# An eighteenth place for expert matrices, one place for overflow matrices, and a reordered expert round

## The reference, cut to what matters

```python
g_sel = jnp.argmax(g_logits, axis=-1)                 # one of 8 groups per token
top_v, top_i = lax.top_k(e_logits, MOE_TOP_K)         # 2 of its 8 experts
gate = p_group[:, None] * jax.nn.softmax(top_v, axis=-1)
...
hid = jax.nn.silu(xb @ w_gate_e[e]) * (xb @ w_up_e[e])   # 64 experts, 1024 -> 256
return hid @ w_down_e[e]                                 # 256 -> 1024
...
return jnp.zeros_like(h2).at[tok].add(ys * wt[:, None])
```

## Time and profile before

| | |
|---|---|
| median of 3 runs | 1522.63 us |
| the profiled execution | 1525.64 us |
| its span, first to last instruction | 1524.0 us |
| PE busy | 1452.7 us (95%) |
| VectorE, ScalarE, GpSimd busy | 526.9, 337.8, 6.7 us |
| DMA over the span | 347.40 MB, mean 228 GB/s |
| mean granted TensorE clock | 0.991 |

### The profile page before, as it was taken

The page is one execution under the profiler, slowest core; times in us unless marked ns, Lnnn a source line. Parts: engine busy times, 40 slices in busy tenths (PEclk is TensorE's granted clock), DMA queues, the critical chain, the costliest instruction groups (busy, mean ns, idle before and its releaser), DMA issues.

```text
span 1524.0 us, 29271 instructions
## 1 busy us (share of the span) xinstructions
PE 1452.7 (95%) x12680; PEld 1232.9 (81%) x12680; DVE 526.9 (35%) x1284; ACT 337.8 (22%) x749; POOL 6.7 (0%) x72
## 2 busy tenths in 40 slices
PE   8999999999999999999999999997999998998887
PEld 6868889978888888888888888886777777776765
DVE  0536164211344430228854541014222332232322
ACT  2153401241100000121555530102111111111111
POOL 0000000000000000000000000000000000000000
PEclk9999999999999999999999999998999999999999
DMA  8333334223444423544334443384999999999995
GB/s 329 132 139 114 135 112 157 70 98 138 138 165 139 149 76 152 231 145 160 115 135 137 141 139 138 138 358 157 420 423 424 423 424 424 424 423 423 424 424 224
DMA packets 58336, 347.40 MB, mean 228 GB/s; under 512 B 12416, under 2 KB 13536, under 8 KB 18656
## 3 DMA queue, kind: packets, MB, share of 16 engines
q1 hardware_dynamic: 55536, 339.20, 57.2%
q10 hardware_dynamic: 2672, 6.33, 1.3%
HBM read 413.21 MB, written 1.49 MB: 272 GB/s over the span
## 4 chain that ended last, share of the span: by engine, by line
PE 88%; DMA 6%; DVE 2%; issue 2%; ACT 1%; SPq 0%; DVEq 0%; ACTq 0%
PE bank L399 37%; PE bank L1049 9%; PE bank L450 9%; PE bank L413 6%; PE bank L1069 5%; PE bank L1080 4%; PE bank L1093 4%; DMA ring<-w_gate_e_dram 4%; PE bank L466 2%; DMA work<-w_gate_e_dram 2%; PE bank L555 1%; PE bank L511 1%; PE bank L927 1%; DVE work L1698 1%; PE bank L701 1%
## 5 line engine op out<-in xcount | busy, mean ns | idle before, releaser
L399 PE MATMUL bank<-hT,ring 128*128 128x256 f32 x2016 | 443.5, 381 | 1.9 <-DVE hT L1698 1.8
L399 PEld LDWEIGHTS bank<-hT,ring 128*128 128x128 f32 x2016 | 382.9, 191 | 56.8 <-issue 6.7
L1707 DVE TENSOR_TENSOR xT<-xT,bank 128x512 f32<-128x512 f32 x100 | 68.8, 688 | 320.7 <-PE bank L1069 210.8
L399 PE MATMUL bank<-work,ring 128*128 128x256 f32 x704 | 153.5, 380 | 0.0
L399 PEld LDWEIGHTS bank<-work,ring 128*128 128x128 f32 x704 | 133.8, 190 | 18.5 <-issue 1.0
L450 PE MATMUL bank<-work,ring 128*128 128x256 f32 x608 | 131.6, 379 | 0.0
L450 PEld LDWEIGHTS bank<-work,ring 128*128 128x128 f32 x608 | 115.8, 190 | 15.4
L1049 PE MATMUL bank<-work 128*32 128x128 f32 x2144 | 113.9, 273 | 11.7 <-issue 9.3
L1049 PEld LDWEIGHTS bank<-work 128*32 128x32 f32 x2144 | 104.3, 110 | 24.0 <-issue 23.6
L1049 PEld LDWEIGHTS bank<-ring,work 128*32 128x32 f32 x1568 | 74.5, 112 | 21.6 <-issue 21.6
L1049 PE MATMUL bank<-ring,work 128*32 128x128 f32 x1568 | 81.4, 278 | 10.5 <-issue 6.8
(11 more groups left out here) (357 smaller groups left out, 1718.7 us busy)
## 6 DMA issues: line engine op xcount, KB each, us to landing
work<-w_up_e_dram SPq DMA_DIRECT2D x33, 1024.0 KB, 23.6
work<-w_down_e_dram SPq DMA_DIRECT2D x33, 1024.0 KB, 26.0
work<-w_gate_e_dram SPq DMA_DIRECT2D x30, 1024.0 KB, 25.8
ring<-w_gate_e_dram SPq DMA_DIRECT2D x26, 1024.0 KB, 26.3
ring<-w_down_e_dram SPq DMA_DIRECT2D x23, 1024.0 KB, 25.1
ring<-w_up_e_dram SPq DMA_DIRECT2D x23, 1024.0 KB, 25.7
ring<-w_up_dram SPq DMA_DIRECT2D x22, 1024.0 KB, 4.9
ring<-w_gates_dram SPq DMA_DIRECT2D x20, 1024.0 KB, 4.9
```

Source lines behind the costliest of these rows:

```text
L399: m = mm(b[:, j * SEQ:(j + 1) * SEQ], w[:, k, j * P:(j + 1) * P], tile(k), start=(k == 0), stop=(k == kt - 1))
L1707: return v.tensor_tensor(dst, a, b, ALU.add)
```

## The change

- The work area is packed again: the routing scratch `rt` moves into `scratch`, `rtx` and `over_add` lie under the place of the expert outputs, `selw_t` under `sel_t`, and the area holds nine 2048-column places for matrices where it held eight. `sq` becomes an expert place as well: 18 places.
- The overflow matrices keep only `hT`. GpSimd's load of turn n now waits for the product of turn n - 1.
- In every round scatter 0 and 1 of the round before stand ahead of gate, and scatter 2 and 3 between gate and up. VectorE adds all four before `gated`.
- During the three waits of the routing TensorE runs 6, 11 and 10 spare products of 128 columns (`keep_running`) into the bank that is written next.
- The last round's down matrices are loaded in halves, first the first half of each, then the second, with a semaphore for each half; `out_of_hidden(r, 0)` waits for the first halves, `out_of_hidden(r, 1)` for the second.
- The output is stored in four parts, each when its additions are done.

```diff
-        wide = area(8704, 8, SLOT)
+        wide = area(6656, 9, SLOT)
...
-        expert_slots = ([wide[:, n, :] for n in range(2, 8)] + [con_sb[:, mask_at:mask_at + SLOT]]
-                        + [ring[(len(UNITS) + n) % RING][:, :] for n in range(RING)] + [wide[:, n, :] for n in range(2)]
-                        + [scratch[:, 0:SLOT]])
+        expert_slots = ([wide[:, n, :] for n in range(3, 9)] + [con_sb[:, mask_at:mask_at + SLOT]]
+                        + [ring[(len(UNITS) + n) % RING][:, :] for n in range(RING)] + [wide[:, n, :] for n in (1, 2)]
+                        + [scratch[:, 0:SLOT], wide[:, 0, :], sq[:, :]])
...
-        over_slots = [hT[:, :, :].rearrange("p k t -> p (k t)"), sq[:, :]]
+        over_slot = hT[:, :, :].rearrange("p k t -> p (k t)")
...
+            def keep_running(times):
+
+                n = len(product)
+                pe.wait_ge(free_sem[n % 8], n // 8)
+                for _ in range(times):
+                    mm(bank[n % 8][:, 0:P], ones, ident, start=True, stop=True)
+
+            keep_running(6)
             pe.wait_ge(S("chosen"), nth("chosen"))
...
+            keep_running(11)
             pe.wait_ge(S("places"), nth("places"))
...
+            keep_running(10)
             pe.wait_ge(S("sel_ready"), 1)
...
+                if r >= 1:
+                    scatter(r - 1, 0)
+                    scatter(r - 1, 1)
                 weights_here("w_gate_e", r)
                 into_hidden("w_gate_e", r, 0)
                 into_hidden("w_gate_e", r, 1)
                 if r == 0:
                     token_rows()
                 if r >= 1:
-                    scatter(r - 1, 0)
-                    scatter(r - 1, 1)
+                    scatter(r - 1, 2)
+                    scatter(r - 1, 3)
                 weights_here("w_up_e", r)
                 into_hidden("w_up_e", r, 0)
                 into_hidden("w_up_e", r, 1)
-                if r >= 1:
-                    scatter(r - 1, 2)
-                    scatter(r - 1, 3)
...
+            overflow_here("w_down_e", GROUPS - 1)
+            for n in range(2):
+                pe.wait_ge(S(f"last_down_landed{n}"), 16 * len(own_experts(GROUPS - 1)))
+                out_of_hidden(GROUPS - 1, n)
...
+                elif u == SLOTS - 3:
+                    sp.wait_ge(product_ready, made("ynt", 7))
                 elif u == SLOTS - 1:
-                    sp.wait_ge(product_ready, made("ynt", 7))
+                    sp.wait_ge(product_ready, made("ssq", 1))
+                elif u == SLOTS - 2:
+                    sp.wait_ge(product_ready, made("out2", 3))
...
+                if (name, r) == ("w_down_e", GROUPS - 1):
+                    sp.dma_start(half_down(expert_slots[u % SLOTS], 0), half_down(A[name][e], 0))\
+                        .then_inc(S("last_down_landed0"), 16)
...
+            for e in own_experts(GROUPS - 1):
+                sp.dma_start(half_down(expert_slots[UNIT_OF["w_down_e", e] % SLOTS], 1), half_down(A["w_down_e"][e], 1))\
+                    .then_inc(S("last_down_landed1"), 16)
             for n in range(4):
+                part = slice(2 * n, 2 * n + 2)
                 sp.wait_ge(bank_free("scatter", GROUPS - 1, n), used("scatter", GROUPS - 1, n))
-            sp.dma_start(out, xT[:, :, :]).then_inc(S("stored"), 16)
+                sp.dma_start(out[:, part, :], xT[:, part, :]).then_inc(S(f"stored{n}"), 16)
...
-                if turn_ >= 2:
-                    pool.wait_ge(product_ready, made(READER[KINDS[(turn_ - 2) % len(KINDS)]], (turn_ - 2) // len(KINDS), 1))
+                if turn_ >= 1:
+                    pool.wait_ge(product_ready, made(READER[KINDS[(turn_ - 1) % len(KINDS)]], (turn_ - 1) // len(KINDS), 1))
```

More of the change, by code:

```diff
@@ L223, in build @@
         selw = area(5376, SEQ)
[L224 to L229, removed]
-        wide = area(8704, 8, SLOT)
+        selw_t = area(5120, SEQ)
+        d_row = area(5632, 2, SEQ)
+        g_row = area(6144, 2, SEQ)
+        rtx = area(3840, 640)
+        over_add = area(4480, EXPERTS)
+        wide = area(6656, 9, SLOT)
         scratch = sb("scratch", [P, 3072])
@@ L234, in build @@
         root2 = scratch[:, 1024:3072]
+        rt = scratch[:, 2048:3072].rearrange("p (t n) -> p t n", t=TT)
         row_buf2 = tmp[0:TT * SSD_HEADS, 1, 0:P]
@@ L310, in expert_weights @@
             if j == OWN:
-                return over_slots[over_turn(name, r) % 2]
+                return over_slot
             return expert_slots[UNIT_OF[name, min(FIRST_OF[r] + j, FIRST_OF[r + 1] - 1)] % SLOTS]
         expert_landed = [S(f"expert_weights_landed{n}") for n in range(SLOTS)]
-        over_landed = [S(f"overflow_weights_landed{n}") for n in range(2)]
+        over_landed = S("overflow_weights_landed")
         def b3(ap, n, inner):
@@ L1038, in weights_here, with overflow_here @@
                     pe.wait_ge(expert_landed[u % SLOTS], 16 * (u // SLOTS + 1))
-                turn_ = over_turn(name, r)
-                pe.wait_ge(over_landed[turn_ % 2], 16 * (turn_ // 2 + 1))
+                overflow_here(name, r)
+            def overflow_here(name, r):
+                pe.wait_ge(over_landed, 16 * (over_turn(name, r) + 1))
             def into_hidden(name, r, n):
@@ L1120, in _ @@
                 turn(r, 1)
-                weights_here("w_down_e", r)
-                out_of_hidden(r, 0)
-                out_of_hidden(r, 1)
+                if r + 1 < GROUPS:
+                    weights_here("w_down_e", r)
+                    out_of_hidden(r, 0)
+                    out_of_hidden(r, 1)
+            overflow_here("w_down_e", GROUPS - 1)
+            for n in range(2):
+                pe.wait_ge(S(f"last_down_landed{n}"), 16 * len(own_experts(GROUPS - 1)))
+                out_of_hidden(GROUPS - 1, n)
             for n in range(4):
@@ L1172, in _, with half_down @@
                     sp.dma_start(pos_sb[:, :], A["pos"]).then_inc(S("late_loads"), 16)
+            def half_down(a, n):
+                return a.rearrange("p (f m) -> p f m", f=2)[:, :, n * 512:(n + 1) * 512]
             ring0 = 7
@@ L1186, in _ @@
                     sp.wait_ge(product_ready, made(READER[before_name], before_r, 1))
-                sp.dma_start(expert_slots[u % SLOTS], A[name][e]).then_inc(expert_landed[u % SLOTS], 16)
+                if (name, r) == ("w_down_e", GROUPS - 1):
+                    sp.dma_start(half_down(expert_slots[u % SLOTS], 0), half_down(A[name][e], 0))\
+                        .then_inc(S("last_down_landed0"), 16)
+                else:
+                    sp.dma_start(expert_slots[u % SLOTS], A[name][e]).then_inc(expert_landed[u % SLOTS], 16)
+            for e in own_experts(GROUPS - 1):
+                sp.dma_start(half_down(expert_slots[UNIT_OF["w_down_e", e] % SLOTS], 1), half_down(A["w_down_e"][e], 1))\
+                    .then_inc(S("last_down_landed1"), 16)
             for n in range(4):
+                part = slice(2 * n, 2 * n + 2)
                 sp.wait_ge(bank_free("scatter", GROUPS - 1, n), used("scatter", GROUPS - 1, n))
-            sp.dma_start(out, xT[:, :, :]).then_inc(S("stored"), 16)
-            sp.wait_ge(S("stored"), 16)
+                sp.dma_start(out[:, part, :], xT[:, part, :]).then_inc(S(f"stored{n}"), 16)
+            for n in range(4):
+                sp.wait_ge(S(f"stored{n}"), 16)
         @block.gpsimd
@@ L1203, in _ @@
                 r, k = turn_ // len(KINDS), turn_ % len(KINDS)
-                if turn_ >= 2:
-                    pool.wait_ge(product_ready, made(READER[KINDS[(turn_ - 2) % len(KINDS)]], (turn_ - 2) // len(KINDS), 1))
+                if turn_ >= 1:
+                    pool.wait_ge(product_ready, made(READER[KINDS[(turn_ - 1) % len(KINDS)]], (turn_ - 1) // len(KINDS), 1))
                 number_of = pool.value_load(be_row[0:1, r:r + 1], min_val=0, max_val=EXPERTS)
                 expert_of = pool.value_load(be_row[0:1, P + r:P + r + 1], min_val=0, max_val=EXPERTS - 1)
-                pool.dma_start(over_slots[turn_ % 2], A[KINDS[k]][bass.ds(expert_of, 1), :, :].rearrange("a p n -> (a p) n"),
-                               cond=(number_of < EXPERTS)).then_inc(over_landed[turn_ % 2], 16)
+                pool.dma_start(over_slot, A[KINDS[k]][bass.ds(expert_of, 1), :, :].rearrange("a p n -> (a p) n"),
+                               cond=(number_of < EXPERTS)).then_inc(over_landed, 16)
         @block.scalar
@@ L2325, in _ @@
             dve.wait_ge(S("dve_step"), nth("dve_step"))
-            slot_of = rtx[:, 560:561]
+            slot_of = sm2[:, 210:211]
             v.tensor_copy(slot_of, con("part")[:, 0:1]).then_inc(S("dve_step"), 1)
@@ L2363, in _ @@
                 if r >= 1:
-                    scattered(r - 1, 0)
-                    scattered(r - 1, 1)
+                    for n in range(4):
+                        scattered(r - 1, n)
                 gated(r, 0)
                 gated(r, 1)
-                if r >= 1:
-                    scattered(r - 1, 2)
```

(1 more changed line is left out.)

## The result

The changed kernel takes **1549.91 us** (median of 4 runs, 1549.29 to 1555.05) against 1522.39 for the kernel before on the same chip (4 runs, 1521.97 to 1524.01). The ratio is 1.0186, 95% interval 1.0163 to 1.0209: slower by 27.5 us, where 1512 was forecast. The profiled execution's span is 1547.6 us, 34.4 more than the 1513.2 of the sum.

A forecast was written before the change was run, and what follows sets the result against it. PE and DMA were taken as nearly level in the expert stage. PE's end, 1515.28 -3.0 start -6.1 waits -1.7 scatter +0.7 turn +0.9 overflow = 1506.1, plus 7.1 gave 1513.2, 10.8 under the span; from median 1522.6: 1512, range 1506 to 1548.

The forecast's parts named there:

- the sum: Whole span: PE side ends at 1506.1 us, DMA side at 1503.4 to 1506.3, plus 7.1 after it: 1513.2.
- One place for the overflow matrix: Ahead of gate and up: skipped load issued one product ahead, x - 0.08 us per use, 43 uses, +0.9 us.
- x: Time a skipped overflow load takes from issue to semaphore: taken as 0.1 us, bounds 0.04 and 1.4.
- Rival A: Ahead of every gate and up: skipped load's semaphore is late and PE becomes the bound; 1545 us, chance 0.26.
- Rival B: Expert stage: x between 0.2 and 0.4, or the issue pauses grow; 1518 to 1524 us, chance 0.10.
- rival D: Expert stage: the pauses shrink, since DMA saturation now ends sooner; 1506 us, chance 0.05.
- Start of the stage: Routing: spare products in three waits hold the clock, speeding gathers and counts; -3.0 us.
- Rival C: Routing: the clock doesn't hold and the spare products run at half clock; 1518 us, chance 0.09.
- Two more places: Matrix loading: two more matrices filled beforehand, -5.0 us for DMA; PE can take only its 6.1 us of waits.
- DMA side: End of loading: last gate landed 1486.5 us, second halves 1501.4 to 1504.3, last down product ending 1503.4 to 1506.3.
- Tail: After the last down product: 8.7 us less 1.6 by storing the output in quarters, 7.1 us.
- the signs listed: Gathers 3.6 us, first gate near 1056.7, no gap ahead of gate or up, last down product ending near 1506.

The follow-up runs named there:

- experiment 3: Changed kernel with two overflow places and 17 expert places, GpSimd still waiting for the product one turn back: 1552.32 us.
- experiment 8: Changed kernel complete, with the wait for the overflow semaphore moved ahead of the waits for the three expert matrices: 1512.87 us.
- experiment 9: Experiment 5 with its added waits for VectorE's addition placed behind the expert-matrix waits, as instructions of their own: 1559.8 us.
- experiment 5: Experiment 1 plus a PE wait for VectorE's first scatter addition, ahead of the expert-matrix waits of gate and up: 1511.59 us.
- experiment 6: Changed kernel, still one overflow place, with the scatters back in the old order (pair behind gate, pair behind up): 1579.87 us.
- experiment 4: Changed kernel without the 27 spare products: 1552.85 us.
- experiment 11: Experiment 2 without the 27 spare products: 1519.13 us.
- experiment 2: Changed kernel with two overflow places and 17 expert places, GpSimd waiting for the product two turns back: 1514.75 us.
- experiment 1: Changed kernel without the overflow loads and PE's waits on them, that part of the computation left out: 1512.36 us.

## Why the prediction was wrong

**The step that failed is "One place for the overflow matrix".** Its price was e per use, the time by which the semaphore comes after the scatter pair. That sum was nearly right: x is 0.13 to 0.16 us (0.1 taken), and the waits for the place are 1.5 us in all (0.9 taken). Of these 0.9 us stand ahead of the last round's down product, which the prediction held to be covered by gathers; the last round has none. But the wait was priced only by when the product may start, not by where PE's instruction stream stands meanwhile. The wait moved from early to just in time, and as an instruction of its own it holds the stream: 0.2 us ahead of the product instead of 2.7. The prediction had named the 22.3 us of pauses of the earlier trace rows and then took them as fixed.

What links the two is the loading of PE's instructions. Count TensorE's instructions in the order of the changed kernel's trace, 26,063 in all: 19 of its pauses in the expert stage, 40.1 of the 41.2 us, stand at the same place in a block of 256 (193 or 194 by this count). The two of the round shown are one block apart: 14 of the gate's last 7 matmuls and their weight loads, 16 of the scatter pair, 224 of 112 matmuls, 254 together, and the waits between them. And 26,063 instructions over the 101 packets of q8 are 258 to a packet. So a pause falls where the next 16.3 KB of instructions begin.

The trace also has the time of each such packet. In the changed kernel the one for the gate's pause (1122.43 to 1124.95) is in flight from 1122.68 to 1123.61, the one for the up product's (1130.49 to 1133.32) from 1130.84 to 1131.89. Over the 19 pauses PE goes on 1.22 to 1.55 us after the packet has landed; in experiments 3, 8 and 9 the same count gives 19, 15 and 19 pauses and 1.23 to 1.59 us. In experiment 8 the packet for the same gate block is in flight from 1115.96 to 1116.89, 2.2 us before PE comes to the block's start at 1118.14 and not 0.25 us after it, and the pause is 0.05 us. The line of q8 (packets, MB, share) in 1122.60 to 1123.65 of the changed kernel, and the same in 1115.90 to 1116.95 of experiment 8; there is none in 1118.93 to 1122.43 of the one and in 1117.0 to 1118.2 of the other:

```profile
q8 instruction: 1, 0.02, 5.5%
```

So the fetch moves with the stream: with the stream 2.5 us less far ahead (as measured in round 2) the packet comes 2.4 us later, measured from PE's arrival at the block. The place of the pauses, what ends them, and that they grow and shrink with the kind of wait are shown (experiments 3, 5, 8, 9). That matrices at 423 GB/s delay the fetch is not: a packet takes 0.98 us in the median in this stage and in the stretches before 1050 us alike, and when a packet was asked for no row shows.

The Trainium skill (Runtime: NRT & Kernel Launch, "Instruction fetch mechanics") says that instructions are refilled in blocks of 16 KiB, 256 instructions, which agrees with the 101 packets, and that the cost of crossing such a boundary is mostly hidden. In this stage it is not: 22.3 us of pauses before, 41.2 after; here the measurement decides.

*The pauses' second price.* After eight of them PE ran part of its work at the lower clock, which cost about 11 us more than before; no term of the sum held that.

*Rival A* gave nearly the right number (1545) by another mechanism: it asked for x of 0.35 us or more and a gap ahead of each gate and up. Neither is there; the gap shows only in the old order (experiment 6). *Rival B* had the right words, "the pauses grow", sized at 12 us at most instead of 37.

*The rest held.* Experiment 8 is the change complete without the hidden stop, and takes 1512.9 us against 1512 forecast. That they agree so closely is partly luck: its last down product ends at 1503.6 us where 1506.1 was forecast, with 6.5 us less of pauses than in the earlier trace rows (rival D) and 5.0 us more of busy time, and the sum had neither. **Start of the stage:** 1055.34 us, 4.4 earlier; but the products before the routing already began 1.7 us earlier in that execution, so 2.7 is the routing's, 3.0 forecast. *Rival C* came true in part: in the changed kernel the clock was at 1.2 GHz from 1037.9 to 1041.3 us and the transposes of `h2` took 3.53 us instead of 1.95, but that was ahead of the spare products, and the gathers ran at the full clock. Over whole runs the spare products are worth 2.9 us (experiment 4) to 4.4 (experiment 11), each uncertain by about 3. **Two more places:** one fewer costs 2.4 us (experiment 2 against 1) or 1.9 (against 8), where one matrix takes 2.5 to load; the intervals overlap, so that this term is not confirmed by itself. **DMA side:** with the pauses smaller the second halves of the last down matrices come last, at 1500.7 us where 1501.4 to 1504.3 was forecast. The end of the chain of experiment 1:

```profile
1487.98 12.71 DMA ring<-w_down_e_dram
...
1500.73 1.92 PE bank L1106 x16
```

**Tail:** 6.9 us behind the last down product, 7.1 forecast. What I had said would prove me wrong, PE standing still ahead of gate in early rounds, did not occur, and the forecast was wrong all the same: the signs listed watched the wait, not the stream.

## What to carry to other kernels

- PE began a new block of instructions no sooner than 1.2 us after its 16.3 KB packet had landed (1.22 to 1.59 us at the 72 pauses counted in four traces).
- Eight of the changed kernel's pauses, 2.5 to 3.4 us long, were followed by work at 1.2 GHz: 32 gather matmuls took 4.65 us, in experiment 9 5.21, instead of 3.59. The pause of 2.52 us at 1122.43 was not: the scatter pair behind it took 1.93.
- In these runs DMA did not keep its rate to the end. In experiment 8 it moves 410 GB/s over the stage but 202 in 1495 to 1498 us, as the kernel before did 240; the 2 KB rows of the halves are not needed for that, and its cause stays open.

```profile
1056.00:1503.57 447.57, 416.03 (x7393) 323.22 (x7384) 126.40 (x323) 80.41 (x216) 2.87 (x65) 0.99 0.98 410
...
1495.00:1498.00 3.00, 2.94 (x110) 2.68 (x103) 0.40 (x2) 0.00 (x0) 0.00 (x0) 1.00 0.52 202
```
